# Gate and up products of two feed-forward layers as seven half-size products for eight, with the weight sums made on GpSimd

## What is computed

```
h = modulate(rmsnorm(x, g_ffn_pre), sh_f, sc_f)
gate, up = h @ w_ffn_gate, h @ w_ffn_up
z = causal_depthwise_conv(gate, w_conv, b_conv)     # three taps along the tokens
y = (silu(z) * up) @ w_ffn_down
```

## Time and profile before

| | us |
|---|---|
| median of 3 runs | 1546.94 |
| lowest and highest run | 1543.73, 1550.08 |
| the profiled execution | 1542.36 |
| its span, first to last instruction | 1540.8 |

### The profile page before, as it was taken

One profiled execution on the slowest core, in us unless ns is written; L12 is line 12 of the kernel. 1 busy time (PEld: TensorE's weight loads), 2 busy tenths in 40 slices (PEclk: granted clock), 3 DMA queues, 4 the chain that ended last, 5 costly groups with the idle time before them and its releaser, 6 DMA issues.

```text
span 1540.8 us, 21126 instructions
## 1 busy us (share of the span) xinstructions
PE 1460.5 (95%) x8356; PEld 931.3 (60%) x8357; DVE 554.0 (36%) x973; ACT 237.6 (15%) x476; POOL 21.7 (1%) x69
## 2 busy tenths in 40 slices
PE   6998999999999999999899999999989999999997
PEld 3875765544444444444485648888448664888843
DVE  1445645111111111111453422224664472222456
ACT  1320003200000000000302530000031052200001
POOL 2000010000000000000000000000000000000000
PEclk9999999999999999999999999999999999999999
DMA  9756545899989999999999054344426933432510
GB/s 374 263 224 228 212 165 200 328 425 422 421 339 413 425 428 426 426 427 424 407 407 370 2 208 175 109 163 187 169 95 244 398 137 109 147 126 85 192 79 28
DMA packets 89969, 400.92 MB, mean 260 GB/s; under 512 B 7040, under 2 KB 12288, under 8 KB 63264
## 3 DMA queue, kind: packets, MB, share of 16 engines
q1 hardware_dynamic: 89888, 399.73, 65.5%
HBM read 398.66 MB, written 1.05 MB: 259 GB/s over the span
## 4 chain that ended last, share of the span: by engine, by line
PE 74%; DMA 10%; DVE 8%; issue 3%; DVEq 3%; ACT 1%; SPq 0%; ACTq 0%
PE psum L1356 20%; PE psum L1029 12%; PE psum L1376 8%; DMA ring<-in_moe_up 7%; PE psum L1177 5%; PE psum L634 4%; PE psum L1325 4%; PE psum L1017 3%; DMA arena<-in_w_mod 2%; PE psum L757 2%; PE psum L563 2%; PE psum L1210 2%; DMA ring<-in_ada_w 1%; PE psum L1195 1%; DVE arena L1875 1%
## 5 line engine op out<-in xcount | busy, mean ns | idle before, releaser
L1029 PE MATMUL psum<-ring,arena 128*64 128x256 f32 (+1 forms) x2240 | 307.3, 427 | 19.9 <-DMA ring<-in_moe_up 9.7
L1356 PE MATMUL psum<-arena,ring 128*128 128x256 f32 x1408 | 304.8, 379 | 0.3
L1356 PEld LDWEIGHTS psum<-arena,ring 128*128 128x128 f32 x1408 | 267.1, 190 | 37.3 <-issue 0.7
L1029 PEld LDWEIGHTS psum<-ring,arena 128*64 128x64 f32 x2240 | 159.8, 137 | 175.8 <-issue 78.4
L1177 PE MATMUL psum<-arena,ring 128*128 128x256 f32 x512 | 112.2, 380 | 0.9 <-DVE arena L1436 0.9
L1788 DVE TENSOR_TENSOR arena<-psum,arena 128x256 f32<-128x256 f32 x32 | 13.6, 425 | 261.1 <-PE psum L1029 261.1
L1177 PEld LDWEIGHTS psum<-arena,ring 128*128 128x128 f32 x512 | 96.8, 190 | 16.1 <-issue 3.1
L1376 PE MATMUL psum<-arena 128*128 128x512 f32 x220 | 102.0, 592 | 0.0
L2023 DVE TENSOR_SCALAR arena<-psum,cols 128x256 f32<-128x256 f32 x44 | 23.9, 544 | 182.8 <-PE psum L1356 182.8
L1017 PE MATMUL psum<-arena 64*128 64x512 f32 x272 | 76.2, 639 | 2.1 <-ACTq L2251 1.4
L1376 PEld LDWEIGHTS psum<-arena 128*128 128x128 f32 x220 | 41.6, 190 | 52.0 <-issue 51.9
(11 more groups left out here) (403 smaller groups left out, 1360.6 us busy)
## 6 DMA issues: line engine op xcount, KB each, us to landing
ring<-in_moe_gate SPq DMA_DIRECT2D x28, 2048.0 KB, 16.1
ring<-in_moe_up SPq DMA_DIRECT2D x28, 2048.0 KB, 14.5
ring<-in_moe_down SPq DMA_DIRECT2D x28, 2048.0 KB, 16.1
arena<-in_w_mod SPq DMA_DIRECT2D x32, 1024.0 KB, 9.4
ring<-in_ada_w SPq DMA_DIRECT2D x12, 2048.0 KB, 10.6
ring<-in_w_qkv SPq DMA_DIRECT2D x12, 2048.0 KB, 15.0
ring<-in_w_ffn_gate SPq DMA_DIRECT2D x10, 2048.0 KB, 9.1
ring<-in_w_ffn_up SPq DMA_DIRECT2D x10, 2048.0 KB, 9.7
```

Source lines behind the costliest of these rows:

```text
L1029: ins = mm(bank[b][o, 0:n], lhsT, w[:, half * n:(half + 1) * n], start=first, stop=last, tile_position=(0, 64 * half))
L1356: last = mm(b[:, k * TOK:(k + 1) * TOK], w[:, c, j * P:(j + 1) * P], hTd[:, c, :], start=(c == 0), stop=(c == DC - 1))
```

## The change

For the first 20 tiles of each layer (`FAST` = 10 pairs) `up_pair(p)` takes the place of `gate_up(2p)` and `gate_up(2p + 1)`. The two tiles of a pair, the two halves of the inner dimension (chunks 0 to 3 and 4 to 7, `lo` and `hi`) and the two halves of the tokens make a 2 x 2 by 2 x 2 block product, for gate (`k` = 0) and up (`k` = 1) alike, and it is made of seven block products for eight. A block product is four products with 128x128 weights and 128 tokens moving. So a pair is 7 x 2 x 4 = 56 products of 128 columns, where two tiles were 32 products of 256 columns. The four results, and partial ones, lie in four PSUM banks, 2 to 5 for even pairs and 6, 7, 0, 1 for odd ones.

- GpSimd makes the weight sums (`s1`, the new `w21`, `s2`, `s4`) of each pair: four instructions on 128 x 1024 floats, one of them in place in the ring. They wait for the slots, and from pair 2 on for the end of pair `p - 2` on TensorE.
- VectorE makes the four sums of `hTd` once a layer (`token_sums`, four instructions on 128 x 512), and seven additions of 128 x 256 in each pair, ahead of and between the conv and gating of the two tiles.
- ScalarE copies the first block product (`p1s`) in each pair; its loop is written out.
- Tiles 20 and 21 stay as they were, in banks 2 and 3. `pair_sums(0)` and `pair_sums(1)` now stand behind these.
- `pair_products` takes the seven terms in another order, with other waits on banks. A semaphore that nobody waited for (`y_state`) is gone.

```diff
+        FAST = NFT // 2 - 1
...
+            for layer in range(2):
+                for p in range(FAST):
...
+                    if p == 0:
+                        pool.wait_ge(S("sum_done"), 7 * layer + 1)
+                    if p == 1:
+                        pool.wait_ge(S("pair_ready"), 67 * layer + 1)
+                    if p >= 2:
+                        pool.wait_ge(S("gu_done"), NFT * layer + 2 * (p - 2) + 2)
...
+                    g(nc.gpsimd.tensor_tensor(s1, w21, w22, ALU.add))
+                    g(nc.gpsimd.tensor_tensor(w21, w11, w21, ALU.subtract))
+                    g(nc.gpsimd.tensor_tensor(s2, s1, w11, ALU.subtract))
+                    nc.gpsimd.tensor_tensor(s4, w12, s2, ALU.subtract).then_inc(S("wsum_ready"), 1)
...
+                def up_pair(p):
...
+                    if p >= 2:
+                        pe.wait_ge(S("act_f"), F0 + 2 * p - 2)
...
+                        for k in range(2):
+                            if p == 0 and b == y0 and slot == 0:
+                                for c in ((0, 1, 2, 3), (4, 5, 6, 7))[k]:
+                                    h_chunk(h_n, c)
+                            for c in range(4):
+                                last = mm(bank[b + k][:, slot * P:slot * P + P], left[:, k, c], right[:, c, :],
+                                          start=(c == 0), stop=(c == 3))
...
+                    product(w11, lo[:, :, 0:P], y0, 0, 0 if p % 2 == 0 else None)
+                    product(w12, hi[:, :, 0:P], x0, 0)
+                    if p == 0 and layer == 0:
+                        flush()
+                    pe.wait_ge(S("wsum_ready"), FAST * layer + p + 1)
+                    product(s4, hi[:, :, P:TOK], x0, 1)
+                    if p == 0:
+                        pe.wait_ge(S("pair_ready"), 67 * layer + 1)
+                    product(s2, hsum[:, 1], y0, 1)
+                    product(w21, hsum[:, 2], y0, 2).then_inc(S("gu_done"), 1)
+                    product(s1, hsum[:, 0], x0, 3)
+                    product(w22, hsum[:, 3], x0, 2, 1 if p % 2 else None).then_inc(S("gu_done"), 1)
...
-                    pair_products(p, (B_N4, B_M5, B_M1, B_M2, B_M6, B_M3, B_N7), None if p % 2 else B_N4, (B_N7,))
+                    pair_products(p, (B_N4, B_M3, B_M6, B_N7, B_M1, B_M5, B_M2), None if p % 2 else B_N4, (B_M2,))
...
+                def up_pair(p):
...
+                    d(V.tensor_tensor(u2, y_[:, :, 1], p1s, ALU.add))
+                    d(V.tensor_tensor(u3, y_[:, :, 2], u2, ALU.add))
+                    dve.wait_ge(S("gu_done"), F0 + 2 * p + 2)
+                    d(V.tensor_tensor(u4, x_[:, :, 3], u2, ALU.add))
+                    d(V.tensor_tensor(x_[:, :, 0], x_[:, :, 0], p1s, ALU.add))
+                    d(V.tensor_tensor(x_[:, :, 1], x_[:, :, 1], u4, ALU.add))
+                    conv(2 * p, bank[x0][:, 0:TOK])
+                    d(V.tensor_tensor(x_[:, :, 3], x_[:, :, 3], u3, ALU.add))
+                    d(V.tensor_tensor(x_[:, :, 2], u3, x_[:, :, 2], ALU.subtract))
+                    gated(2 * p, bank[x0 + 1][:, 0:TOK])
+                    conv(2 * p + 1, bank[x0][:, TOK:2 * TOK])
+                    gated(2 * p + 1, bank[x0 + 1][:, TOK:2 * TOK])
```

More of the change, by code:

```diff
@@ L1339, in _, with product @@
                 F0 = NFT * layer
+                def up_pair(p):
+                    n = n0 + 2 * (p // 2)
+                    w11, w12, w21, w22 = pair_weights(n0, p)
+                    s1, s2, s4 = (wsum[p % 2][:, i] for i in range(3))
+                    y0, x0 = ((2, 4), (6, 0))[p % 2]
+                    if p >= 2:
+                        pe.wait_ge(S("act_f"), F0 + 2 * p - 2)
+                    if p == 1:
+                        pe.wait_ge(S("rows_copied"), 8 + 4 * layer)
+                        pe.wait_ge(S("mod_copied"), 7 + 2 * layer)
+                    if p % 2 == 0:
+                        for k in range(2):
+                            pe.wait_ge(S(f"slot{(n + k) % RING}_loaded"), 16 * ((n + k) // RING + 1))
+                    def product(left, right, b, slot, freed=None):
+                        for k in range(2):
+                            if p == 0 and b == y0 and slot == 0:
[4 more added lines that the diff above has]
+                                          start=(c == 0), stop=(c == 3))
+                                if freed == k and c == 0:
+                                    last.then_inc(S("slot_freed"), 1)
+                        return last
+                    lo, hi = hTd[:, 0:4], hTd[:, 4:8]
+                    product(w11, lo[:, :, 0:P], y0, 0, 0 if p % 2 == 0 else None)
[10 more added lines that the diff above has]
+                    product(w22, hsum[:, 3], x0, 2, 1 if p % 2 else None).then_inc(S("gu_done"), 1)
@@ L1380, in pair_products @@
                             last.then_inc(S("ffn_terms"), 1)
-                for f in range(NFT):
+                for p in range(FAST):
+                    up_pair(p)
+                for f in range(2 * FAST, NFT):
                     gate_up(f)
[L1384 to L1387, removed]
                 for p in range(PAIRS - 2):
-                    pair_products(p, (B_N4, B_M5, B_M1, B_M2, B_M6, B_M3, B_N7), None if p % 2 else B_N4, (B_N7,))
+                    pair_products(p, (B_N4, B_M3, B_M6, B_N7, B_M1, B_M5, B_M2), None if p % 2 else B_N4, (B_M2,))
                 first, rest = (B_N4, B_M5, B_M3, B_M1, B_N7), (B_M2, B_M6)
@@ L2068, in combine @@
                     d.to(tt(bank[4], tb, bank[B_M6], ALU.add), "sum_done")
-                for f in range(NFT):
-                    conv(f)
-                    if f == 1 and layer == 0:
-                        mod_columns()
-                        gain_ready(2, 8, col("g_mix_pre", 8, 8))
-                    if f in (18, 19):
-                        pair_sums(f - 18)
+                token_sums()
+                if layer == 0:
+                    mod_columns()
+                    gain_ready(2, 8, col("g_mix_pre", 8, 8))
+                for p in range(FAST):
+                    up_pair(p)
+                for f in range(2 * FAST, NFT):
+                    dve.wait_ge(S("gu_done"), F0 + f + 1)
+                    conv(f, bank[2 + f % 2][:, 0:TOK])
+                    gated(f, bank[2 + f % 2][:, TOK:2 * TOK])
+                    pair_sums(f - 2 * FAST)
                 for p in range(2, PAIRS):
```

66 lines of the change are left out of this document (44 added, 22 removed).

## The result

The changed kernel took 1518.08 us (median of 4 runs, 1514.03 to 1522.30), the one before 1545.34 us (median of 4, 1539.31 to 1550.08). The ratio is 0.984, with a 95% interval of 0.9817 to 0.9863. The forecast was 1523.5 us against 1546.94, a ratio of 0.985, and its range of 1515 to 1535 holds the time. The profiled execution took 1517.28 us where that of before took 1542.36: 25.1 us less, for a forecast of 23.4 (1519.0).

The account below looks back on a forecast made before the run. TensorE's own work, 95% busy, was taken to bound the kernel. Two layers of -13.3 (passes), +1.0 (start) and +0.6 us (end) make -23.4 us off the median 1546.94: 1523.5 us, range 1515 to 1535.

Parts of the forecast that it names:

- TensorE's passes: Gate and up: 1120 passes of 128 columns at 111.7 ns replace 640 of 256 columns; 13.3 us less per layer.
- Start of a layer: First gate and up products wait for more chunks of `hTd`: 1.0 us later per layer; token sums hidden by 1.6 us.
- Weight sums on GpSimd: Gate and up pairs: 2.2 us an instruction, 9.1 us a pair, hidden behind TensorE's 12.5 us.
- VectorE and ScalarE: Gate and up pairs: seven additions of 0.43 us on VectorE, ten more short ScalarE copies; hidden but for the end.
- The end: End of gate and up: `pair_sums(1)` comes late for the down products, a new wait of 0.6 us per layer.
- The sum: Whole kernel: 2 x (-13.3 + 1.0 + 0.6) = -23.4 us; profiled execution 1519.0 us, median 1523.5 us.
- GpSimd in VectorE's way: Gate and up pairs: both engines block each other at SBUF, 16.0 us a pair, kernel 1586 us; chance 0.09 including slow GpSimd.
- Part of the gain lost: Gate and up: passes nearer 116 ns or waits at the first pairs, 4.8 us a layer, kernel 1533 us; chance 0.13.
- loads not overlapped: Gate and up: weight load and product add up to 220 ns a pass, kernel about 1765 us; chance 0.01.
- Full seven eighths: Gate and up: a 128-column pass costs half a 256-column one, 108.2 ns, kernel 1516 us; chance 0.04.

Follow-up runs that it names:

- The run with 96 columns: Changed kernel with every product of `up_pair` taken on 96 of its 128 tokens, all weight loads kept: 1518.83 us (one run).
- the split alone: Kernel before, with each gate and up product taken as two of 128 tokens, eight for eight, no sums: 1552.81 us, ratio 1.0069.
- The run with seven: Changed kernel with GpSimd making three of its four weight sums per pair twice, seven instructions a pair: 1598.47 us (one run).
- The run with mended ends: Changed kernel with `pair_sums(0)` ahead of the last pair, `pair_sums(1)` behind tile 20, and later waits for chunks 6 and 7: 1515.31 us, ratio 0.9827.
- the run with two inputs: Changed kernel with four unused 128 x 256 VectorE additions more at each pair's head, both inputs in SBUF: 1532.85 us (one run).

## Why the prediction was right, point by point

**TensorE's passes.** Forecast 111.7 ns and 13.3 us less per layer; measured 111.7 ns and, since the old passes started every 215.8 ns and not every 216.3, 13.1 us. This was the term that mattered, and it came from a dozen passes in a quite different place of the program. Half of the old distance would have given some 4 us too much per layer. The run with 96 columns and the row with 128x36 weights show the reason given for it, the weight load, to be the true one, and the split alone shows its price. The reason is worth less than the prediction had it, though: without the load a pass of 128 columns takes 109.2 ns, not 108.2, so the load costs 2.5 ns a pass. The rule that a weight load overlaps running products only in another row group (the Trainium skill, "TensorE: Matmul & The Clock Gate", section "Packing small matmuls") would have made passes of 220 ns, by the prediction's estimate; 2240 passes here say 111.7.

**Start of a layer.** Forecast 1.0 us. From VectorE's first instruction of `evac_h` to the first down product layer 1 took 152.8 us before (1311.82 to 1464.62) and 140.8 after (1298.01 to 1438.80): 12.0 less. With 13.1 gained by the passes the start cost 1.1: the first pass starts 1.53 us behind `evac_h`'s start and not 0.69, and the ninth then comes 0.23 late. So nearly all of the 0.3 by which 12.0 falls short of the forecast's 12.3 lies in the passes, and not in the start. The token sums ended as forecast, and TensorE did not wait for them.

**Weight sums on GpSimd.** Forecast 2.2 us an instruction between ends of 1.2 and 2.9; measured 2.36, with 2.43 from start to start. 9.7 us a pair for 9.1, hidden as said. The run with seven, at 16.9 us a pair, confirms the price of a GpSimd that is late; no run came nearer to the threshold of 12.5 than 9.7 and 16.9. Doubling a one-input instruction of the same engine came out 7% low. Whether the two inputs are the reason was not tested, so that it came so near may be luck; anything below 3.1 would have hidden.

**VectorE and ScalarE.** 0.43 us an addition as forecast, and hidden, also with four more of them in a pair.

**The end.** Forecast 0.6 us per layer, measured 0.65: 66.34 us from the first down product to the last in both layers, for 65.70. The run with mended ends takes it away by moving just what the prediction named.

**The sum.** By the traces the change is worth 2 x (-12.0 + 0.65) = -22.7 us, for a forecast of -23.4; 2.4 us more came by scatter of stretches that the change does not touch. That the profiled executions differ by nearly the forecast is in part this luck.

**The rivals.** GpSimd in VectorE's way: the exclusion is real, but not for instructions with one input in PSUM, which all those of a pair are; the conclusion that gave it 0.09 held. The reason as written did not quite: it sets them apart from L1424 as having "at most one input" in SBUF, but L1424 has only one tensor input as well, and differs in that it has nothing in PSUM. Its price, the full length of every instruction in every pair, was not tested as it stands; the run with two inputs shows that collisions can cease after a few pairs. Part of the gain lost, loads not overlapped: neither. Full seven eighths: not met, and with 109.2 ns for the columns alone it could not have been.

## What to carry to other kernels

Seven products for eight pays on a TensorE that does nothing else, but with halved products each pass costs more than half: of 12.5% only 9.5% are left (13.1 us of 138.1). Of the 4.2 us missing in a layer some 1.4 are the fixed part of more passes (109.2 ns for half of 215.8), and 2.8 the weight load, which at 111.7 ns is the floor. Price such a change by passes of the very form it will have, found anywhere in the trace, not by a share of the old ones. Extra sums cost nothing here on either of two engines that had the time for them. Additions of VectorE with one input in PSUM ran beside GpSimd's without waiting, those with two in SBUF did not. Look at the ends of the stretch, where the cover of moved work is thinnest.

## What the runs showed of the hardware that I had not expected

- Collisions ended by themselves. The 40 additions with two SBUF inputs took VectorE 38.5 us a layer for the 17 they need alone, but TensorE lost only 8, because the engines fell into an order in which the two hardly met any more.
- After waits of 2.5 to 4.5 us TensorE's clock was granted at its lower level and passes of 128 columns took 213 ns, twice the 106.7 that 128 columns take at 2.4 GHz; there the pass takes 111.7, the load's time. A pass bound by its load at the full clock still got 1.9 times as long.
- The load of 128x128 weights and the pass of 128 columns are almost the same length, 111.7 and 109.2 ns, so halving 256 columns to 128 meets the load's floor by 2.5 ns only.
